# Two transformer blocks in fp32 on one Trainium2 core: norm sums regrouped or folded on VectorE, one modulation made later, other PSUM banks for the last products

## What is computed

```
mod = c @ w_ada + b_ada; sh1, sc1, gt1, sh2, sc2, gt2 = split(mod)
h = rms(x, g_pre_mix) * (1 + sc1) + sh1;   proj = h @ w_in
merged = sigmoid(ga) * (short_conv @ w_proj_conv) + sigmoid(gb) * (stick_breaking @ w_proj_attn)
mix_out = merged @ w_out
x = x + gt1 * rms(mix_out, g_post_mix)              # norm 0
h2 = rms(x, g_pre_mlp) * (1 + sc2) + sh2            # norm 1
ff = relu(h2 @ w_mlp_in)**2 @ w_mlp_out
x = x + gt2 * rms(ff, g_post_mlp)                   # norm 2
# second block
z = rms(x, attn_norm) @ w_in_2;  mix = [conv_mixer(z), nsa_attention(z)]
x = x + mix @ w_out_2
gate, up = split(rms(x, ffn_norm) @ w_gate_up)      # the ffn norm
x = x + (silu(gate) * up) @ w_down
return rms(x, final_norm)
```

## Time and profile before

| | us |
|---|---|
| median of 3 runs | 799.14 (796.7 to 805.18) |
| the profiled execution | 798.94 |
| its span in the trace | 797.2 |
| PE busy | 747.5, 94% |
| DVE busy | 502.4, 63% |
| ACT busy | 370.5, 46% |
| POOL busy | 76.3, 10% |
| mean granted clock of PE | 0.955 of full |

### The profile page before, as it was taken

One profiled execution on the slowest core, in us unless ns is written; L12 is line 12 of the kernel. 1 busy time (PEld: TensorE's weight loads), 2 busy tenths in 40 slices (PEclk: granted clock), 3 DMA queues, 4 the chain that ended last, 5 costly groups with the idle time before them and its releaser, 6 DMA issues.

```text
span 797.2 us, 13936 instructions
## 1 busy us (share of the span) xinstructions
PE 747.5 (94%) x6075; PEld 722.4 (91%) x6075; DVE 502.4 (63%) x599; ACT 370.5 (46%) x508; POOL 76.3 (10%) x75
## 2 busy tenths in 40 slices
PE   4499999999979999999998999999799999999997
PEld 3499989999969999999997999797599999999997
DVE  4888678687446786653436589964754766564441
ACT  3353444443434545544344455577654544444441
POOL 1500111001000000000005000004000231221000
PEclk9599999999969999999998989999899999999998
DMA  9979766785413886666561561333424576555501
GB/s 349 371 242 339 242 215 218 254 288 189 159 53 114 259 265 209 211 213 197 173 194 26 159 212 54 105 108 103 161 64 149 171 251 197 182 192 177 177 31 53
DMA packets 123825, 146.00 MB, mean 183 GB/s; under 512 B 3988, under 2 KB 114804, under 8 KB 123764
## 3 DMA queue, kind: packets, MB, share of 16 engines
q1 hardware_dynamic: 122400, 143.32, 54.7%
q10 hardware_dynamic: 1364, 1.79, 0.7%
HBM read 144.05 MB, written 1.05 MB: 182 GB/s over the span
## 4 chain that ended last, share of the span: by engine, by line
PE 73%; DVE 14%; issue 5%; ACT 4%; DMA 2%; POOL 1%; POOLq 0%; SPq 0%; ACTq 0%; DVEq 0%
PE bank L581 62%; DVE w_lo L1435 4%; DVE mod_acc L1427 3%; ACT w_hi L1053 3%; PE bank L627 2%; DVE wide L1719 2%; DMA raw<-in_w_ada 2%; PE bank L608 1%; DVE score L1803 1%; DVE neg_max L1785 1%; PE bank L616 1%; PE bank L837 1%; PE bank L896 1%; PE bank L798 1%; PE bank L818 1%
## 5 line engine op out<-in xcount | busy, mean ns | idle before, releaser
L1435 DVE TENSOR_TENSOR w_lo<-raw,w_hi 128x2048 fp32r<-128x2048 f32 (+1 forms) x108 | 244.2, 2265 | 139.0 <-ACT w_hi L1053 138.7
L1053 ACT ACTIVATE w_hi<-raw 128x2048 fp32r<-128x2048 f32 (+1 forms) x110 | 206.6, 1883 | 225.3 <-PE bank L581 198.5
L581 PE MATMUL bank<-act_hi,w_hi 128*128 128x256 f32 x816 | 233.3, 286 | 5.9 <-ACT act_hi L1209 2.7
L581 PE MATMUL bank<-act_hi,w_lo 128*128 128x256 f32 x816 | 230.4, 282 | 1.7 <-DVE w_lo L1435 1.7
L581 PE MATMUL bank<-act_lo,w_hi 128*128 128x256 f32 x816 | 230.6, 283 | 0.8 <-DVE act_lo L1695 0.4
L581 PEld LDWEIGHTS bank<-act_hi,w_hi 128*128 128x128 f32 x816 | 157.2, 193 | 8.2 <-issue 6.7
L581 PEld LDWEIGHTS bank<-act_lo,w_hi 128*128 128x128 f32 x816 | 157.1, 192 | 1.9 <-DVE act_lo L1695 0.7
L581 PEld LDWEIGHTS bank<-act_hi,w_lo 128*128 128x128 f32 x816 | 156.6, 192 | 2.3 <-DVE w_lo L1435 2.3
L581 PE MATMUL bank<-hidden_hi,w_hi 128*128 128x256 f32 x432 | 121.3, 281 | 0.9 <-DVE wide L1982 0.9
L581 PE MATMUL bank<-hidden_hi,w_lo 128*128 128x256 f32 x432 | 121.1, 280 | 0.0
L581 PE MATMUL bank<-hidden_lo,w_hi 128*128 128x256 f32 x432 | 121.1, 280 | 0.0
(11 more groups left out here) (263 smaller groups left out, 928.6 us busy)
## 6 DMA issues: line engine op xcount, KB each, us to landing
raw<-in_w_in SPq DMA_DIRECT2D x31, 1024.0 KB, 5.6
raw<-in_w_ada SPq DMA_DIRECT2D x24, 1024.0 KB, 6.7
raw<-in_w_gate_up SPq DMA_DIRECT2D x22, 1024.0 KB, 5.1
raw<-in_w_mlp_in SPq DMA_DIRECT2D x16, 1024.0 KB, 5.7
raw<-in_w_mlp_out SPq DMA_DIRECT2D x16, 1024.0 KB, 5.4
raw<-in_w_out SPq DMA_DIRECT2D x8, 1024.0 KB, 6.1
raw<-in_w_down SPq DMA_DIRECT2D x8, 1024.0 KB, 5.1
raw<-in_w_down SPq DMA_DIRECT2D x4, 768.0 KB, 4.3
```

Of the source, the lines that this page charges most:

```text
L581: i = e.matmul(dst, lhs, rhs, start=start and k == 0 and m == 0 and n == 0, stop=stop and k == kt - 1 and n == 2, skip_group_check=True)
L1053: e.activation(w_hi[slot][:, 0:kt * n_cols], raw[i % N_RAW][:, 0:kt * n_cols], ACT.Copy).then_inc(hi_split, 1)
L1435: e.tensor_tensor(w_lo[slot][:, 0:kt * n_cols], raw[i % N_RAW][:, 0:kt * n_cols], w_hi[slot][:, 0:kt * n_cols].bitcast(F32), ALU.subtract) ...
```

## The change

1. In the projection PC, behind the first tile of the first bank, PE waits for `rms_set` (long set) and does one matmul of the identity by itself, 128x128 in plain fp32 (`keep_busy(1, ...)`), into bank SUMS.
2. Norm 0: DVE adds the squares of pairs 1 and 2 to those of pair 0 (`add_to_first`, 128x512 each, before and behind the split of OUT1+2's partner). PE sums only pair 0 and pair 3, both behind OUT1+3. Nothing stands between OUT1+2 and OUT1+3 any more.
3. Behind the spread of norm 0 stand 8 such identity matmuls, behind each of the four column sums of norm 1 one, and behind the spread of norm 1 five. Their target is the bank that MLP1 takes next.
4. GATE2's chunks stand behind MLP1+7, +10, +13 and +17 in the plan. Its sum is made in two halves of 4 matmuls each, inside the third product of w_mlp_out's first output: one ahead of its first tile, one ahead of its second. DVE takes it off behind the split that follows the second of those products. Its bank is now asked for behind the first output's, so the banks of the later ones move by one.
5. Norm 2: as norm 0, DVE adds pairs 1 and 2 to pair 0, behind the second products of outputs three and four; PE sums pair 0 and pair 3 behind the last product.
6. The ffn norm: behind its pair additions DVE also adds tiles 2 and 4 to tile 0 (128x256 each). PE sums tile 0 and tile 6 only, ahead of the seventh and of the eighth tile of the interleaved GU and GU+1. The sums behind OUT2+2, OUT2+3 and GU+1 are gone.
7. The ring of w_down is 1, 2, 0, so its four outputs get banks 0, 1, 2, 0.

```diff
+        GATE2_WITH = tuple(MLP1 + 7 + i * 10 // (ADA_CHUNKS - 1) for i in range(ADA_CHUNKS))
...
-            if n % 2 and (n < 6 * ADA_CHUNKS or MLP1 + 2 <= n < MLP1 + 2 + 2 * ADA_CHUNKS):
+            if n % 2 and n < 6 * ADA_CHUNKS or n in GATE2_WITH:
                 plan_ada()
...
+        DOWN_RING = [1, 2, 0]
-        banks.ring = [0, 1, 2]
+        banks.ring = DOWN_RING
...
+            def keep_busy(n, o):
+
+                for _ in range(n):
+                    e.matmul(o[:, 0:P], ident[:], ident[:], start=True, stop=True, skip_group_check=True)
...
+                            if p == PC and j == 0 and k == 0:
+                                pe.wait_ge(rms_set, 1)
+                                keep_busy(1, bank[SUMS])
...
             product(OUT1 + 2, start_bank(OUT1 + 2), act_hi, act_lo, ready_merged)
+            product(OUT1 + 3, start_bank(OUT1 + 3), act_hi, act_lo, ready_merged)
             pe.wait_ge(rms_set, 1)
-            sum_columns(0, 0)
-            sum_columns(1, 0)
-            product(OUT1 + 3, start_bank(OUT1 + 3), act_hi, act_lo, ready_merged)
-            sum_columns(2, 0)
+            sum_columns(0, 0, ready=(pair_added, 2))
             sum_columns(3, 0)
             spread_rstd(0)
+            o, o1 = start_bank(MLP1), start_bank(MLP1 + 1)
+            keep_busy(8, o)
             pe.wait_ge(col_rms, 1)
             for i in range(DT // 2):
                 sum_columns(i, 1)
+                keep_busy(1, o)
             spread_rstd(1)
+            keep_busy(5, o)
...
-                if p == GATE2_SUM_AFTER:
-                    modulation_sum(GATE2)
+            def gate2_half(half):
+                modulation_sum(GATE2, range(half * DT // 2, (half + 1) * DT // 2))
+
...
-                            start=(r == 0), stop=(r == PARTS - 1))
-                if i >= 2:
-                    if i == 2:
-                        pe.wait_ge(col_rms, 2)
-                    sum_columns(i - 2, 2)
-            sum_columns(2, 2)
-            sum_columns(3, 2)
+                            start=(r == 0), stop=(r == PARTS - 1), between=gate2_half if (i, r) == (0, 2) else None)
+            pe.wait_ge(col_rms, 2)
+            sum_columns(0, 2, ready=(pair_added, 4))
+            sum_columns(DT // 2 - 1, 2)
...
             def ffn_sums(i):
-                sum_tiles((2 * i,), i == 0, i == DT // 2 - 1, (pair_added, i + 1))
+
+                if i == 0:
+                    pe.wait_ge(cmp_copied, 2)
+                sum_tiles((i * (DT - 2),), i == 0, i == 1, (pair_added, 4 + DT // 2 + 1 + i))
...
-                if i >= 2:
-                    if i == 2:
-                        pe.wait_ge(cmp_copied, 2)
-                    ffn_sums(i - 2)
...
-                    two_products(GU, b, b_up, ffn_hi, ffn_lo, ready_ffn)
-                    ffn_sums(DT // 2 - 2)
-                    ffn_sums(DT // 2 - 1)
+                    two_products(GU, b, b_up, ffn_hi, ffn_lo, ready_ffn, between=ffn_sums)
...
+            def add_to_first(i, n):
+
+                dve.wait_ge(squared, squared_by[n] + i)
+                dve.wait_ge(pair_added, n + i - 1)
+                e.tensor_tensor(squares[:, 0:2, :], squares[:, 0:2, :], squares[:, 2 * i:2 * i + 2, :],
+                                ALU.add).then_inc(pair_added, 1)
...
+                if i == DT // 2 - 2:
+                    dve.wait_ge(pair_added, 4 + DT // 2 - 1)
+                    for k in (2, 4):
+                        dve.wait_ge(pair_added, 4 + DT // 2 - 2 + k // 2)
+                        e.tensor_tensor(squares[:, 0, :], squares[:, 0, :], squares[:, k, :], ALU.add).then_inc(pair_added, 1)
```

More of the change, by code:

```diff
@@ L473, in build @@
         banks.use(("rstd", 1), h2_scaled, DT)
-        GATE2_SUM_AFTER = MLP1 + 2 * ADA_CHUNKS + 1
         for i in range(FT // 2):
             banks.use(MLP1 + i, relu_set, i + 1)
-            if MLP1 + i == GATE2_SUM_AFTER:
-                banks.use(("mod", GATE2), mod_set, 6)
         for i in range(DT // 2):
             banks.use(("mlp_out", i), branch2_set, 2 * i + 2)
+            if i == 0:
+                banks.use(("mod", GATE2), mod_set, 6)
         banks.use(("rstd", 2), *residual_at(1, "times", DT // 2 - 1))
@@ L584, in passes, with product, two_products @@
                     i.then_inc(product_done, 1)
-            def product(p, o, hi, lo, ready, k0=0, start=True, stop=True, tokens_first=False):
+            def product(p, o, hi, lo, ready, k0=0, start=True, stop=True, tokens_first=False, between=None):
                 for k in range(tiles_of(p)[0]):
+                    if between is not None and k < 2:
+                        between(k)
                     passes(p, o, hi, lo, ready, k, k0, start, stop, tokens_first)
-            def two_products(p, o, o1, hi, lo, ready):
+            def two_products(p, o, o1, hi, lo, ready, between=None):
                 for k in range(DT):
+                    if between is not None and k >= DT - 2:
+                        between(k - DT + 2)
                     passes(p, o, hi, lo, ready, k, 0, True, True)
@@ L601, in transpose_rows, with modulation_sum @@
                             ident[first:first + n, first:first + n]).then_inc(rows_turned, 1)
-            def modulation_sum(v):
+            def modulation_sum(v, columns_=range(DT)):
                 o, acc = start_bank(("mod", v)), mod_acc[v % 2]
@@ L606, in modulation_sum @@
                 pe.wait_ge(consts, 1)
-                for k in range(DT):
+                for k in columns_:
                     i = e.matmul(o[:, k:k + 1], acc[:, k * P:(k + 1) * P], ones[:, 0:1], start=True, stop=True,
                                  skip_group_check=True)
-                i.then_inc(mod_summed, 1)
+                if k == DT - 1:
+                    i.then_inc(mod_summed, 1)
             def sum_tiles(tiles, first, last, ready):
@@ L619, in sum_tiles, with sum_columns @@
                     i.then_inc(sums_done, 1)
-            def sum_columns(i, n):
+            def sum_columns(i, n, ready=None):
                 pe.wait_ge(consts, 3)
-                pe.wait_ge(squared, squared_by[n] + i)
+                if ready is not None:
+                    pe.wait_ge(*ready)
+                else:
+                    pe.wait_ge(squared, squared_by[n] + i)
                 for tt in range(TT):
@@ L1621, in vector_program @@
             e.tensor_tensor(scale2[:], scale2[:], cols("g_pre_mlp", 0, DT), ALU.mult).then_inc(gains_set, 1)
+            add_to_first(1, 0)
             low_after(product_at[OUT1 + 2])
+            add_to_first(2, 0)
             def column_reciprocal(n):
@@ L1689, in vector_program @@
                         low_after(product_at[MLP2 + i * PARTS + r])
+                    if (i, r) == (0, 1):
+                        modulation(GATE2)
+                        dve.wait_ge(mod_set, 6)
+                        e.tensor_tensor(gain2[:], mod[:, GATE2 * DT:], cols("g_post_mlp", 0, DT),
+                                        ALU.mult).then_inc(gains_set, 1)
+                    elif r == 1 and i >= 2:
+                        add_to_first(i - 1, 2)
             def attn_parts(i):
```

11 lines of the change are left out of this document (4 added, 7 removed).

## The result

Over 20 runs each the changed kernel takes 788.79 us in the median (785.55 to 799.14), the one before 799.05 (794.38 to 805.67): a ratio of 0.9871, 95% interval 0.9849 to 0.9893, that is 10.3 us less where 12.6 were forecast. A further set of it, 11 runs beside 28 others of before, gave 794.86 for 799.00, a ratio of 0.9936 (0.9902 to 0.9970), which is 4 to 5 us less. The two intervals do not overlap, and what differs between the two sets no run shows. Two runs of the changed kernel (799.14 in the first set, 801.54 in the further one) were in a slow state and are left out of the ratios; the others lie between 785.55 and 798.14, 12.6 us apart. The profiled execution has a span of 788.9, against 797.2.

What follows compares the result with a forecast made beforehand. The prediction took PE, busy 94% of the span, as the bound, with two paces of product matmuls. Its terms, −0.3 −2.5 −5.7 −0.8 −3.3 = −12.6 us, gave 786.3 us, range 780.5 to 796.

Steps and rivals of the forecast that it cites:

- rival 1: PE's pace does not come out fast; only removed work and stalls count: −6.0, 793.0 us; chance 0.22.
- PC's identity matmul: Projection PC: the matmul may flip the slow pace, but most of the gain is slack; −0.3 us.
- Norms 0 and 1: Removed sums of norm 0 gain 1.5 us, identity matmuls' effect on the clock 1.0; −2.5 us together.
- The step on the clock: Norm 1 and start of MLP1: identity matmuls help PE's clock a little, taken −1.0 us; full help −5.6.
- upper bound of +2.2: Norms: identity matmuls that do nothing for the clock only queue and cost +2.2 us at most.
- The MLP: 864 matmuls at the fast pace −3.6, fewer records −0.8 and −0.9, w_lo stall −0.4; −5.7 us.
- flip and flip back: MLP: the GATE2 sum's two halves cancel, so 864 matmuls run at 113.7 ns; −3.6 us.
- Norm 2's tail: End of norm 2: 24 records of column sums become 16; −0.9 us.
- The ffn norm: Fewer records −0.9, pace −0.4, stall gone −0.5, DVE's extra additions ahead of w_lo +1.0; −0.8 us.
- w_down: New ring removes the wait for bank 2, −0.9, and the fast pace runs on, −2.4; −3.3 us.
- Rival 2: An odd flip in the norms starts MLP1 slow and fast stretches turn slow: 800.1 us; chance 0.06.
- rival 4: DVE falls behind in the MLP and ffn norm, PE waits 0.9 us repeatedly: +4.1, 790.4 us; chance 0.09.

Runs made afterwards that it cites:

- the new ring alone: The kernel before with only the ring of w_down changed to 1, 2, 0: 798.10 us, ratio 0.9995.
- the old ring's trace: The changed kernel with the ring of w_down put back to 0, 1, 2: 792.75 us, ratio 0.9941.
- late halves: The changed kernel with the GATE2 sum's halves ahead of the fourth and fifth tile instead of the first and second: 788.7 us, ratio 0.9894.
- one group: The changed kernel with the whole GATE2 sum in one group ahead of the fourth tile: 790.42 us, ratio 0.9921.
- the short pairs: Changed kernel, whole GATE2 sum then an identity matmul; one one-column matmul, then an identity matmul, in MLP1+2 and GU+4: 786.72 us, ratio 0.9863.
- the third experiment: The kernel before plus one identity matmul ahead of the second tile of MLP1+10: 797.35 us, ratio 0.9994.

## Why the prediction was right, and where not

*The direction* held in both sets. *The size* held in the first: −12.6 forecast, −10.3 measured, and −8.3 in the profiled execution, inside the range. In the further set it is −4 to −5, inside the range too but under half of the forecast, nearer to rival 1's −6.0. That the first came so near is in part luck, since the mechanism of the largest term, the MLP's pace, did not hold.

*PC's identity matmul*, −0.3. It flips the pace as assumed, but both ways: in the traces with it the stretch before came slow or fast by chance, and what it gains or loses is 0.35 us of the time to the SHIFT2 sum (36.4 or 36.75), the rest of that stretch being held by DVE and ACT, as the forecast had it.

*Norms 0 and 1*, −2.5. Measured −2.6 in the first trace and −3.2 in the means (35.0 for 38.2). The step on the clock held in size (1.4 for 1.0, by one trace), and in part in mechanism: in the first trace and four others the eight matmuls keep the clock up for some 3 us and it falls between the sums, at 227 where it was 224. The forecast had it low already when the eight begin, up behind them, and low again behind the next groups; that is what three other traces show. Its upper bound of +2.2 for matmuls that only queue adds up to 2.4 (4 × 0.4 and 2.0 − 1.2), and the term did not use it.

*The MLP*, −5.7 with norm 2. The step that failed is "flip and flip back" for the two halves, which should have kept 666 matmuls fast: behind the first half the pace is slow, and the second does not turn it back. Of the 3.6 for the pace 0.9 came, since 666 matmuls were slow for 864 (198 × 4.5 ns). The 8 records gave their 0.8, and the rest of the −3.0, 1.3, are the waits on `w_lo` at 272 and 284, which are gone (−0.4 was forecast). Norm 2's tail, −0.8 for −0.9, held. But the start of the MLP was slow in four of ten traces with the change, so that gain too comes and goes.

*The ffn norm*, −0.8. With w_out_2 at the fast pace, as before, the stretch takes 143.31 against 144.25, −0.9: held, with the new wait on `w_lo` at 0.65 to 0.89 from start to start where +1.0 was put in. In the profiled execution w_out_2 was slow (+0.6). In three of the ten traces gate and up started slow, and where no pair followed they and w_down took 6.8 us more. With the old ffn sums the wait of 0.6 on `w_lo` behind GU+1 stands after the last group and ended in the fast pace in four traces of four, each time behind a slow row. The change has its last wait ahead of two groups that cancel, mostly behind a fast row, and 1,370 matmuls behind it take what that one wait leaves: of the stretches this one differs most between the traces with the change.

*w_down*, −3.3: −1.1 and −2.4 in the traces. The stall of 1.18 stands in all three traces with the old ring and in none of the eleven with the new. The pace held in this comparison, and the runs of the new ring alone show no gain in the median, not even the stall's 1.1, which the interval does not exclude.

*The attention's* +2.8 was in no step. It goes with the clock. Windows of PE, all instructions, of the changed kernel in its first and its second trace:

```profile
556.00:560.00 4.00, 4.00 (x16) 0.50 1.09 343
560.00:564.00 4.00, 3.40 (x22) 0.50 0.04 14
564.00:568.00 4.00, 4.00 (x21) 0.50 0.00 0
```

```profile
556.00:560.00 4.00, 2.47 (x12) 0.50 1.10 348
560.00:564.00 4.00, 4.00 (x21) 0.50 0.67 213
564.00:568.00 4.00, 3.40 (x30) 0.86 0.00 0
```

PE is at half clock for 14 us in the one and 10 in the other; before it was 7. The time does not follow in proportion: 147.49, 144.73 and 144.66 us. In the second trace PE stood idle for the first part of the 10. In all fourteen traces the stretch took 143.7 to 148.2, with and without the change, and the old ring's trace has the longest.

*The rivals.* Rival 2, the wrong start, is real, and not an outcome of the program but of single executions; it had 0.06. Rival 1's 793.0 lies between the two sets of runs of the changed kernel. Of rival 4 one wait of the kind is seen: in three of the four traces with the sum moved and a fast row ahead, PE waits for `w_lo` in the third product of w_mlp_out, from start to start 1.15 (late halves), 1.14 (one group) and 0.78 us (the short pairs); in the changed kernel's first trace it is 0.25, between the halves. No wait of the kind stands in the traces with a slow row ahead, so part of what a fast pace gains is lost there. By the Trainium skill's one gap for one width ("TensorE: Matmul & The Clock Gate", section "Back-to-back issue gap") the paces would be nil; every trace here shows two, 113.4 and 117.8 ns at a granted clock of 1.00, and the identity matmul of the third experiment turns one into the other. As to the Trainium skill's section "HAM oscillation — how this bites in real kernels" of the same page, which blames idle gaps: the matmuls in the gaps did not hold the clock. In the first trace a gap of 0.9 us was left at 224 and the clock fell at 227.2; in the second it fell at 227.2 too, with PE busy all through 222 to 228.

## What to carry to other kernels

Divide the long pieces of the chain by their counts before costing any edit: a pace that differs by 4% is worth more than most stalls, and one small group of other matmuls can decide it for a thousand. A term that rests on such a state is no sure gain, since a stall ahead may set it anew; price the removed instructions and waits apart from it, and take several profiles and several sets of runs before believing either. Where a kernel shows two paces, a one-column matmul and, a tile later, one of 128 columns cost 0.5 us and led to the fast one in 11 of 12 cases here.

## What I had not expected

Two paces of PE at one granted clock (113.4 and 117.8 ns for 128x256 with its load of weights), which persist over 100 us and turn on one inserted matmul. One program in two executions differed by some 3 us in the MLP and 3 in the attention; between kernels with the same program in gate, up and w_down these differed by up to 6.8, and two sets of runs of one kernel gave ratios of 0.9871 and 0.9936.
